# Differential attention in a two-layer trunk: GpSimd makes the subtraction factors, the reciprocals move between two maxima, a ScalarE copy moves between the exponentials

## The chip, the cores and the metric

The kernel runs on one core of one Trainium2 chip. The metric is the device time of one execution in microseconds (us). Its engines are named as the profile names them: PE (TensorE matmuls, PEld its weight loads), DVE (VectorE), ACT (ScalarE), POOL (GpSimd) and SP (the queue that issues the weight loads from HBM). Each engine runs its own list of instructions in order. They meet at semaphores.

## The reference

Two layers over 128 context tokens and 512 latent tokens, width 1024. Each layer has a token mixer with three parts side by side (6 heads of differential attention, a short convolution, 6 heads of latent attention, MLA below), and then a feed-forward part, dense in layer 0 and with experts in layer 1. The change is in the differential attention only:

```python
def diff_attention(q, k, v, lam):
    scale = DA ** -0.5                                # DA = 32, V_A = 64
    def block(qb):
        s = jnp.einsum('bqhcd,bkhcd->bhcqk', qb, k).astype(F32) * scale
        p = jax.nn.softmax(s, axis=-1)
        w = p[:, :, 0] - lam * p[:, :, 1]             # two softmaxes for each head
        return jnp.einsum('bhqk,bkhe->bqhe', w.astype(v.dtype), v)
    return sweep_query_blocks(block, q)
```

The kernel doesn't normalise the two softmaxes one by one. With sums S0 and S1 of the exponentials E0 and E1 it forms E0 + CNEG * E1, where CNEG = (1/S1) * S0 * (-lam), multiplies that by V, and scales the small output by 1/S0.

## The kernel before

**Items.** One loop over `k` from -2 to 60 runs in each layer on PE, ACT and DVE (`mixer_pe`, `mixer_act`, `mixer_dve`), with its own order of work on each. An item `j` is one head and one tile of 128 queries. Items 0 to 29 are differential (6 heads of 5 tiles, two scores each, c = 0 and 1). Items 30 to 59 are MLA heads with one score each. The tiles of a head come in the order 1, 2, 3, 4, 0. Tile 0 is the context: its scores have 128 columns, and those of a latent tile 640.

**The pipeline.** In step `k` an engine does its part for several items at once. PE: the scores of item k+2 (L1763), one group of transposes for the next head (`turn_group`, L1968), the product of item k-1 with V (L1791, 10 matmuls for a latent tile), the transposes of item k's weights (L1968, from `E`), and in one step of five a second group. ACT: the copy of the transposed group out of PSUM (`turn_out`, L759, into `QT` or `KT`), the two exponentials of item k+2 (L805), the copy `PT` (L810), and the copy of the second group where there is one. DVE: the two maxima of item k+2 (L1157), then for item k+1 the reciprocal `RC` (L1166), the factor `CNEG` (L1169) and the combination of `E` (L1171), then the scaling of item k-1's output (L1180), and after it work that is spread over certain steps (`latents_scale`, L1128, in steps 0 to 2 and 4 to 6, `latents_root` in step 3, `modulation_out` in step -1 of layer 0).

**What orders them.** There are two score buffers in PSUM. Score n waits until the exponential of score n-2 has given its sum (`exp_ready`), and a maximum waits for its score. All transposed groups of the attention go through one PSUM bank, so a group waits for the copy of the group before it (`turn_out`). The first score of a head waits for all six groups of that head. Groups 0, 1, 2, 4 and 5 are turned one in each step, in front of the product with V (`groups_at(k, 0)`), and group 3 in the third step of a head, at the step's end. Groups 0 to 2 come from the stack `QS`, 3 to 5 from `KS`.

**GpSimd.** POOL makes these stacks (`stack(h, k)`, L572 to L585): each is two casts and then two subtractions of the whole width. `QS` has two buffers, `KS` one, and a stack waits until the former contents have been turned. It also rotates the MLA queries and keys (`latent_rope`, L535 to L541). Its list is: stacks of head 0, query stack of head 1, ropes, key stack of head 1, the rope of the last key tile, and then the stacks of heads 2 to 5. That last rope waits for DVE's `latents_scale` of steps 0 to 2. In `Chain.then` an engine waits for its own instruction before it goes on.

## Time and profile before

| what | value |
|---|---|
| median of 3 runs | 2131.0 us (2129.53 to 2131.98) |
| the profiled execution, its own time | 2139.79 us |
| its span in the profile | 2137.8 us |
| busy over the span | PE 1907.5 us (89%), PEld 1719.2 us (80%), DVE 1417.2 us (66%), ACT 1031.7 us (48%), POOL 278.0 us (13%) |
| mean granted TensorE clock | 0.945 |

The differential items of layer 0 take the stretch from 217.92 to about 322 us, those of layer 1 start at 1168.88 us. The profiled execution is one of its own and was 8.8 us slower than the median of the runs. Busy shares are averages over stages that differ: PE is busy 89% of the whole span and less in the stretches of the change.

### The profile page before, as it was taken

To read this page: it belongs to the slowest core of one execution; us is meant where nothing else is said; L and a number is where in the kernel's file an instruction comes from. 1 tells how busy PE (TensorE), PEld (TensorE's weight loads), DVE (VectorE), ACT (ScalarE), POOL (GpSimd) and SP (SyncE) were. 2 spreads that over 40 slices of the span, in tenths; PEclk is the share of its full clock that TensorE was granted. 3 is DMA by queue.
4 is the path that set the end of the run, shared out by engine and by line. 5 is a ranking of instruction groups with operands and counts; after the bars stand their busy time and mean duration, and the time that the engine had idled before them with its cause. 6 is when DMAs were issued, how large, how long until landed. Compare 5 with 4: busy or idle time off the path is not lost.

```text
span 2137.8 us, 28644 instructions
## 1 busy us (share of the span) xinstructions
PE 1907.5 (89%) x11291; PEld 1719.2 (80%) x11291; DVE 1417.2 (66%) x2033; ACT 1031.7 (48%) x1388; POOL 278.0 (13%) x411
## 2 busy tenths in 40 slices
PE   5988789897999999997996889885699999999994
PEld 3986678797999999997985778774488888888883
DVE  5466784436665666546557884434589888898887
ACT  4235686413221121223235676414477777777772
POOL 0074310100111111000254311002000000000002
PEclk9999799798999999998997899987799999999997
DMA  8225200033555555421120000004789999999996
GB/s 325 66 75 201 79 1 1 20 99 99 175 176 163 170 164 185 127 89 39 57 94 26 1 1 1 1 1 176 296 349 384 405 390 404 392 400 397 376 396 225
DMA packets 115910, 375.64 MB, mean 176 GB/s; under 512 B 8640, under 2 KB 66400, under 8 KB 89408
## 3 DMA queue, kind: packets, MB, share of 16 engines
q1 hardware_dynamic: 94448, 303.50, 38.0%
q0 software_dynamic: 14240, 51.49, 7.1%
q10 hardware_dynamic: 7088, 18.81, 2.3%
q8 instruction: 91, 1.49, 0.3%
q14 instruction: 43, 0.35, 0.1%
HBM read 347.13 MB, written 26.64 MB: 175 GB/s over the span
## 4 chain that ended last, share of the span: by engine, by line
PE 75%; DVE 11%; ACT 8%; DMA 3%; issue 2%; POOL 1%; SPq 0%; ACTq 0%; DVEq 0%; POOLq 0%
PE PS L1988 31%; PE PS L1929 25%; PE PS L1968 5%; PE PS L1675 5%; PE PS L1791 4%; PE PS L1763 3%; ACT E L805 3%; ACT PT L810 1%; DMA rows_of_slots<-HTM,SLI 1%; DVE KCn L1128 1%; DMA araw<-in_w_ada_head 1%; DVE split L1402 1%; DVE SS L1111 1%; DMA raw<-in_w_ada_head 1%; DVE NT__177 L1458 1%
## 5 line engine op out<-in xcount | busy, mean ns | idle before, releaser
L1988 PE MATMUL PS<-H,split 128*128 128x320 f32 x2688 | 401.5, 312 | 10.3 <-DVE H L1595 8.0
L1988 PEld LDWEIGHTS PS<-H,split 128*128 128x128 f32 x2688 | 399.5, 190 | 12.5 <-issue 10.6
L976 ACT CAST split<-raw 128x2048 fp32r<-128x2048 f32 (+2 forms) x64 | 112.8, 1763 | 266.9 <-PE PS L1988 229.4
L1402 DVE TENSOR_TENSOR split<-raw,split 128x2048 fp32r<-128x2048 f32 (+2 forms) x64 | 138.0, 2161 | 129.6 <-ACT split L976 129.2
L1320 DVE TENSOR_TENSOR split<-raw,split 128x2048 fp32r<-128x2048 f32 x82 | 186.9, 2290 | 50.9 <-ACT split L931 50.9
L1320 DVE TENSOR_TENSOR msplit<-raw,msplit 128x2048 fp32r<-128x2048 f32 x82 | 187.8, 2292 | 32.7 <-ACT msplit L931 32.5
L1929 PE MATMUL PS<-split,HT 128*128 128x512 f32 x816 | 196.7, 397 | 5.4 <-DVE HT L1299 5.4
L1929 PE MATMUL PS<-msplit,HT 128*128 128x512 f32 x816 | 190.6, 389 | 0.0
L931 ACT CAST split<-raw 128x2048 fp32r<-128x2048 f32 x82 | 157.1, 1916 | 68.0 <-PE PS L1929 44.9
L931 ACT CAST msplit<-raw 128x2048 fp32r<-128x2048 f32 x82 | 156.9, 1914 | 64.6 <-PE PS L1929 64.6
L1675 PE MATMUL PS<-split,H 128*128 128x384 f32 (+1 forms) x960 | 170.2, 339 | 15.3 <-DVE split L1402 12.0
L1675 PEld LDWEIGHTS PS<-split,H 128*128 128x128 f32 x960 | 168.4, 194 | 17.0 <-DVE split L1402 13.2
L1929 PEld LDWEIGHTS PS<-split,HT 128*128 128x128 f32 x816 | 152.6, 190 | 36.6 <-DVE HT L1299 5.8
L1929 PEld LDWEIGHTS PS<-msplit,HT 128*128 128x128 f32 x816 | 153.2, 188 | 31.8
L1157 DVE TENSOR_REDUCE NM<-PS 128x1 f32<-128x640 f32 (+1 forms) x180 | 125.0, 714 | 71.8 <-PE PS L1763 70.0
L1988 PE MATMUL PS<-ACTB,split 128*128 128x320 f32 x1056 | 155.4, 309 | 0.0
L1988 PEld LDWEIGHTS PS<-ACTB,split 128*128 128x128 f32 x1056 | 155.0, 188 | 0.0
L805 ACT ACTIVATE E<-PS,NM 128x640 f32<-128x640 f32 (+1 forms) x180 | 126.8, 710 | 37.6 <-DVE NM L1157 37.5
L1511 DVE SCALAR_TENSOR_TENSOR DOTS<-DOTW,CROW 128x1024 f32<-128x1024 f32 x112 | 137.0, 1223 | 4.9
L1561 DVE SCALAR_TENSOR_TENSOR xT<-PS,MOD,xT 128x128 f32<-128x128 f32 (+2 forms) x120 | 43.5, 432 | 136.0 <-PE PS L1988 136.0
L1988 PE MATMUL PS<-MIX,split 128*128 128x320 f32 x768 | 117.2, 316 | 2.6 <-DVE MIX L1220 2.6
L1988 PEld LDWEIGHTS PS<-MIX,split 128*128 128x128 f32 x768 | 116.7, 194 | 3.1 <-DVE MIX L1220 3.1
(299 smaller groups left out, 2860.4 us busy)
## 6 DMA issues: line engine op xcount, KB each, us to landing
raw<-in_moe_w_gate SPq DMA_DIRECT2D x55, 1024.0 KB, 7.2
raw<-in_moe_w_down SPq DMA_DIRECT2D x55, 1024.0 KB, 8.1
raw<-in_moe_w_up SPq DMA_DIRECT2D x54, 1024.0 KB, 7.3
DOTW<-in_w_ada_rows POOLq DMA_DIRECT2D x56, 512.0 KB, 4.5
raw<-in_w_ada_head SPq DMA_DIRECT2D x16, 1024.0 KB, 6.8
mraw<-in_moe_w_up SPq DMA_DIRECT2D x14, 1024.0 KB, 7.2
mraw<-in_moe_w_gate SPq DMA_DIRECT2D x13, 1024.0 KB, 7.3
mraw<-in_moe_w_down SPq DMA_DIRECT2D x13, 1024.0 KB, 8.1
```

What stands on the lines that cost most here:

```text
L805: A.activation(out, src, ACT.Exp, bias=NM[:, m:m + 1], accum_out=SM[:, m:m + 1]).then_inc(S["exp_ready"], 1)
L931: A.copy(msplit[n % M_SPLIT][:, 0, :], mraw[n % M_RAW]).then_inc(S["pieces_hi"], 1)
L976: A.copy(split[u % 2][:, 0, 0:w], src[:, 0:w]).then_inc(S["split_hi"], 1)
L1157: V.tensor_reduce(NM[:, m:m + 1], src, op=ALU.max, axis=ax, negate=True).then_inc(S["max_ready"], 1)
L1320: V.tensor_tensor(msplit[n % M_SPLIT][:, 1, :], mraw[n % M_RAW], msplit[n % M_SPLIT][:, 0, :].bitcast(f32), ALU.subtract).then_inc(S["piec ...
L1402: V.tensor_tensor(split[u % 2][:, 1, 0:w], src[:, 0:w], split[u % 2][:, 0, 0:w].bitcast(f32), ALU.subtract).then_inc(S["split_lo"], 1)
L1511: ins = V.scalar_tensor_tensor(out=DOTS[:, :], in0=w[:, :], scalar=1.0, in1=CROW[:, v, :], op0=ALU.mult, op1=ALU.mult, accum_out=MOD[:, l, ...
L1675: ins = T.matmul(PS[:, m % 8, 0:w_], H[:, a, 4 * half + k, t * P:(t + 1) * P], W[:, w, k, :], start=(half == 0 and k == 0 and w == 0 and a ...
L1791: ins = T.matmul(PS[:, 0, 0:VA_W], PT[j % 2][:, i * P:(i + 1) * P], V[:, kt, col:col + VA_W], start=(i == 0), stop=(i == len(tiles) - 1))
L1929: ins = T.matmul(PS[:, bank + hf, :], A[:, a, 2 * j + k, :], W[:, w, first:first + 512], start=(j == 0 and k == 0 and a == 0 and w == 0), ...
L1968: return T.transpose(out, in_, ident[0:in_.shape[0], 0:in_.shape[0]])
L1988: ins = T.matmul(PS[:, 4 * (u % 2) + 2 * c + hf, 0:HALF], W[:, w, k, c * P:(c + 1) * P], A[:, a, k, hf * HALF:(hf + 1) * HALF], start=(k = ...
```

## The change

- **DVE.** The reciprocal of item k+1 (new function `invert`) stands between the two maxima of item k+2 in place of behind them, and DVE doesn't wait for its end; it signals the new semaphore `inverted`. In steps whose new item is an MLA item, `invert` stands for MLA items where the reciprocal stood. DVE no longer computes `CNEG`. It waits for the new semaphore `quotients` before the combination.
- **POOL.** It computes `CNEG` for each of the 30 differential items, when `inverted` allows. Between these, the stacks of heads 2 to 5 are made in halves: casts in one step, subtractions in the next. Keys of the coming head go with its first two steps, queries of the head after it with steps 3 and 4. The rope of the last key tile goes behind the factor and the half stack of step 3.
- **ACT.** The copy of the group in place 0 stands in front of the last exponential of item k+2. For two-score items this is between the two exponentials. For MLA items it is where it was.

```diff
--- before.py
+++ after.py
@@ -346,7 +346,7 @@
                  "setA_free setB_free proj_ready proj_free "
                  "nsq_ready nsq_used root_ready x_root eps_ready normed roped cache_loaded stores "
                  "ct_turned ct_hi ct_lo lat_ready lat_q lat_k subln_gained "
-                 "q_stacked k_stacked turned turn_out scored max_ready exp_ready w_ready pt_ready pt_out o_ready o_stored "
+                 "inverted quotients q_stacked k_stacked turned turn_out scored max_ready exp_ready w_ready pt_ready pt_out o_ready o_stored "
                  "subln_sq subln_sum subln_root subln_done mix_turned mix_hi mix_lo conv_hi conv_lo act_ready act_hi act_lo "
                  "router_loaded router_hi router_lo logits_ready logits_out top_ready top_exp gates_ready "
                  "crow_in crow_ready dot_used dots zeroed tables_ready h_rows_ready rows_turned rows_out mask_ready rank_ready slots_ready owners_ready scattered "
@@ -570,19 +570,21 @@
                 pool.dma_start(O["new_mla_ckv"][0, l], CN[:, 0, Q_RANK:Q_RANK + KV_RANK]).then_inc(S["stores"], 16)
                 pool.dma_start(O["new_mla_krope"][0, l], CN[:, 0, Q_RANK + KV_RANK:C_W]).then_inc(S["stores"], 16)
                 stores += 32
-                def stack(h, k):
+                def stack(h, k, halves=(0, 1)):
 
                     former = 6 * h if k else 6 * (h - 2) + 3
-                    if former > 0:
+                    if former > 0 and 0 in halves:
                         pool.wait_ge(S["turned"], l * TURNS + former)
                     buf, stack_, hi, lo = ((QA, QS[h % 2], (0, 2), (1, 3)), (KA, KS, (0, 1), (2, 3)))[k]
                     src = buf[:, :, h * 2 * DA:(h + 1) * 2 * DA].rearrange("p t (c d) -> p t c d", c=2)
-                    nc.gpsimd.tensor_copy(stack_[:, :, :, hi[1], :].bitcast(f32r), src)
-                    ch.then(nc.gpsimd.tensor_copy(stack_[:, :, :, hi[0], :].bitcast(f32r), src))
-                    for row in lo:
-                        ins = nc.gpsimd.tensor_tensor(stack_[:, :, :, row, :].bitcast(f32r), src,
-                                                      stack_[:, :, :, 0, :], ALU.subtract)
-                    ins.then_inc(S["k_stacked" if k else "q_stacked"], 1)
+                    if 0 in halves:
+                        nc.gpsimd.tensor_copy(stack_[:, :, :, hi[1], :].bitcast(f32r), src)
+                        ch.then(nc.gpsimd.tensor_copy(stack_[:, :, :, hi[0], :].bitcast(f32r), src))
+                    if 1 in halves:
+                        for row in lo:
+                            ins = nc.gpsimd.tensor_tensor(stack_[:, :, :, row, :].bitcast(f32r), src,
+                                                          stack_[:, :, :, 0, :], ALU.subtract)
+                        ins.then_inc(S["k_stacked" if k else "q_stacked"], 1)
 
                 def latent_rope(t, k):
                     pool.wait_ge(S["normed"], l * 21 + 2 * NT + 2 * t + k + 1)
@@ -601,10 +603,19 @@
                 latent_rope(NT - 1, 0)
                 pool.wait_ge(S["stores"], stores)
                 stack(1, 1)
-                latent_rope(NT - 1, 1)
-                for h in range(2, HEADS):
-                    stack(h, 0)
-                    stack(h, 1)
+                for k in range(-1, A_ITEMS - 1):
+                    j = k + 1
+                    m = 2 * (j % 3)
+                    pool.wait_ge(S["inverted"], l * A_ITEMS + j + 1)
+                    nc.gpsimd.tensor_scalar(CNEG[:, j % 3:j % 3 + 1], RC[:, m + 1:m + 2], SM[:, m:m + 1], LAM[:, l:l + 1],
+                                            ALU.mult, ALU.mult).then_inc(S["quotients"], 1)
+                    h, i = (k + 2) // NT + 1, (k + 2) % NT
+                    if 1 < h < HEADS and i in (0, 1):
+                        stack(h, 1, (i,))
+                    if 1 <= h < HEADS - 1 and i in (2, 3):
+                        stack(h + 1, 0, (i - 2,))
+                    if k == 3:
+                        latent_rope(NT - 1, 1)
 
                 pool.wait_ge(S["o_stored"], l * ITEMS + A_ITEMS)
                 for t in range(NT):
@@ -788,12 +799,13 @@
             root(HEADS, QK)
 
             for k in range(-2, ITEMS):
-                if (hg := groups_at(k, 0)) is not None:
-                    turn_out(*hg)
+                hg = groups_at(k, 0)
                 if k + 2 < ITEMS:
                     j = k + 2
                     cols = KEYS if TILE_ORDER[j % NT] else P
                     for c in range(comps_of(j)):
+                        if c == comps_of(j) - 1 and hg is not None:
+                            turn_out(*hg)
                         n = score_of(j, c)
                         bank, m = 2 + 2 * (n % 2), 2 * (j % 3) + c
                         act.wait_ge(S["max_ready"], l * SCORES + n + 1)
@@ -1143,6 +1155,17 @@
                         latents_scale(t - 1, 1)
                 latents_sums(t)
 
+            def invert(j):
+                m, n = 2 * (j % 3), comps_of(j)
+                dve.wait_ge(S["exp_ready"], l * SCORES + score_of(j, n - 1) + 1)
+                if j >= 3:
+                    dve.wait_ge(S["o_stored"], l * ITEMS + j - 2)
+                ins = V.reciprocal(RC[:, m:m + n], SM[:, m:m + n])
+                if n == 2:
+                    ins.then_inc(S["inverted"], 1)
+                else:
+                    ch.then(ins)
+
             for k in range(-2, ITEMS + 1):
                 if k + 2 < ITEMS:
                     j = k + 2
@@ -1156,18 +1179,15 @@
                             src, ax = PS[:, bank, 0:P], AX.X
                         V.tensor_reduce(NM[:, m:m + 1], src, op=ALU.max, axis=ax, negate=True).then_inc(
                             S["max_ready"], 1)
+                        if c == 0 and k >= -1 and comps_of(k + 1) == 2:
+                            invert(k + 1)
                 if 0 <= k + 1 < ITEMS:
                     j = k + 1
                     m, cols = 2 * (j % 3), KEYS if TILE_ORDER[j % NT] else P
-                    dve.wait_ge(S["exp_ready"], l * SCORES + score_of(j, comps_of(j) - 1) + 1)
-                    if j >= 3:
-                        dve.wait_ge(S["o_stored"], l * ITEMS + j - 2)
-                    n = comps_of(j)
-                    ch.then(V.reciprocal(RC[:, m:m + n], SM[:, m:m + n]))
-                    if n == 2:
-
-                        ch.then(V.tensor_scalar(CNEG[:, j % 3:j % 3 + 1], RC[:, m + 1:m + 2], SM[:, m:m + 1],
-                                                LAM[:, l:l + 1], ALU.mult, ALU.mult))
+                    if comps_of(j) == 1:
+                        invert(j)
+                    else:
+                        dve.wait_ge(S["quotients"], l * A_ITEMS + j + 1)
                         V.scalar_tensor_tensor(out=E[:, j % 3, 0, 0:cols], in0=E[:, j % 3, 1, 0:cols],
                                                scalar=CNEG[:, j % 3:j % 3 + 1], in1=E[:, j % 3, 0, 0:cols],
                                                op0=ALU.mult, op1=ALU.add).then_inc(S["w_ready"], 1)
```

## Rows read from the trace of the kernel before

**Rows 1.** By stretch: span; busy of PE, PEld, DVE, ACT, POOL; PEclk; DMA; GB/s.

```profile
217.92:237.36 19.44, 14.00 (x76) 11.74 (x77) 13.45 (x32) 12.71 (x29) 2.36 (x3) 0.68 0.68 216
237.36:260.30 22.94, 15.89 (x107) 14.09 (x105) 17.03 (x43) 13.07 (x31) 11.12 (x18) 0.85 0.00 1
...
276.02:291.75 15.73, 13.77 (x106) 11.92 (x105) 13.75 (x31) 12.76 (x31) 5.99 (x9) 1.00 0.00 1
```

**Rows 2.** Chain that ended last, stretch 218 to 345: start us, us, what.

```profile
293.05 0.58 ACT QT L759
293.63 1.57 ACT E L805 x4
...
296.28 0.58 ACT QT L759
```

**Rows 3.** Timeline of PE, stretch 288 to 332: start us, us, instruction [idle before].

```profile
292.42 0.60 PE L1968 MATMUL PS<-ident,QS 128*128 128x128 f32 x4
292.85 1.26 PE L1791 MATMUL PS<-VA,PT 128*128 128x64 f32 x10
293.94 0.71 PE L1968 MATMUL PS<-ident,E 128*128 128x128 f32 x5
294.48 0.56 PE L1763 MATMUL PS<-KT,QT 128*128 128x320 f32 x2
```

**Rows 4.** Timeline of DVE, stretch 300 to 332.

```profile
301.32 1.54 DVE L1157 TENSOR_REDUCE NM<-PS 128x1 f32<-128x640 f32 x2
302.79 0.15 DVE L1166 RECIPROCAL RC<-SM 128x2 f32<-128x2 f32 x1
302.98 0.27 DVE L1169 TENSOR_SCALAR CNEG<-RC,SM,LAM 128x1 f32<-128x1 f32 x1
303.29 0.89 DVE L1171 SCALAR_TENSOR_TENSOR E<-E,CNEG 128x640 f32<-128x640 f32 x1
304.12 0.28 DVE L1180 TENSOR_SCALAR QA<-PS,RC 128x64 f32<-128x64 f32 x1
```

**Rows 5.** Timeline of PE, stretch 215 to 262.

```profile
237.36 0.83 PE L1763 MATMUL PS<-KT,QT 128*128 128x320 f32 x4
242.63 1.11 PE L1968 MATMUL PS<-ident,QS 128*128 128x128 f32 x4 [4.44 <-POOL QS L583]
...
246.49 1.22 PE L1763 MATMUL PS<-KT,QT 128*128 128x320 f32 x4
```

**Rows 6.** Timeline of POOL, stretch 205 to 262.

```profile
237.91 0.73 POOL L535 TENSOR_TENSOR rope_c<-KCn,ROPE 128x96 f32<-128x96 f32 x2 [17.56 <-DVE KCn L1128]
...
240.91 1.67 POOL L583 TENSOR_TENSOR QS<-QA,QS 128x320 fp32r<-128x320 f32 x2
...
243.56 1.95 POOL L583 TENSOR_TENSOR KS<-KA,KS 128x384 fp32r<-128x384 f32 x2
...
246.37 1.70 POOL L583 TENSOR_TENSOR QS<-QA,QS 128x320 fp32r<-128x320 f32 x2
```

**Rows 7.** Timeline of DVE, stretch 215 to 262.

```profile
234.26 0.54 DVE L1128 SCALAR_TENSOR_TENSOR KCn<-KCn,RT,GR 128x96 f32<-128x96 f32 x2
...
246.23 0.17 DVE L1458 TENSOR_TENSOR NT__177<-RT 128x6 f32<-128x6 f32 x1
246.43 0.83 DVE L1459 SCALAR_TENSOR_TENSOR NT__177<-NT__177,SS 128x6 f32<-128x6 f32 x1
```

**Rows 8.** Timeline of ACT, stretch 215 to 262.

```profile
220.83 1.28 ACT L805 ACT_TABLE_LOAD   x1
```

**Rows 9.** Timeline of ACT, stretch 0 to 60.

```profile
20.09 1.28 ACT L1003 ACT_TABLE_LOAD   x1
25.65 0.21 ACT L1003 ACTIVATE XROOT<-XMEAN 128x5 f32<-128x5 f32 x1 [4.27 <-DVE XMEAN L1480]
```

**Rows 10.** Groups by line and shape, POOL, whole span: xcount, busy us, mean ns, idle before.

```profile
L535 POOL TENSOR_TENSOR rope_c<-QC,ROPE 128x96 f32<-128x96 f32 x16 | 6.0, 395 | 35.6 <-DVE QC L1128 35.6
...
L645 POOL MEMSET TIO<- 128x1 f32 x17 | 0.6, 98 | 0.0
```

## Prediction

> **What bounds the kernel now.** I read the page first (PE is the busiest engine of the whole span), then busy time by stretch, one head at a time, since the change touches 30 of the 60 items of each layer. A steady head lasts 15.73 us [rows 1]. PE is busy for 13.77 of it, DVE for 13.75, ACT for 12.76: nothing is full, so engines wait for each other in a circle. The stretch of the first head's items lasts 19.44 us with a granted clock of 0.68, the second 22.94 us, 7.2 more than a steady one.
>
> The chain shows the circle [rows 2]: group copy 0.58, exponentials with their sums 1.57, second score of the next item 0.56, group of transposes 0.43 [rows 3], hand-offs 0.1, and the next group copy: 3.24 us from one copy to the next. ACT waits for a group that PE can only turn behind a score, which waits for ACT's last exponential. PE's own work in such a step is 0.43 + 1.09 + 0.54 (starts that follow each other in [rows 3]) + two scores at 0.54 = 3.14 us. DVE's own is close as well: two maxima 1.47, reciprocal 0.19, `CNEG` 0.31, combination 0.83, scaling about 0.20, sum 3.00 [rows 4].
>
> The second head's loss has one large piece. PE stood still for 4.44 us before the first query group of head 2, until POOL's L583 ended [rows 5]. POOL had sat 17.56 us before the last key rope, and the stack stands behind that rope in its list [rows 6]. From the first score of that step to that of the next are 9.13 us [rows 5].
>
> **Part by part.** Per layer; the two layers have the same loop, and I take them as equal.
>
> *First head, ACT's table.* The load of the exponential's table takes 1.28 us at 220.83, behind the first group copy and directly in the path [rows 8]. With the copy moved, the exponential is the first instruction of the loop on ACT. A load doesn't wait for what its activation waits for: one ran at 20.09 and its activation came 4.27 us after the load, when DVE was ready [rows 9]. So it goes into idle time, and the first exponential also no longer stands behind the 0.58 copy. That is 1.28 + 0.58 plus the wait for the group, about 2.4 us at the first exponential; a bit more is won at the next two steps, where the old circle of copy and scores ran at a low clock, and some lost to POOL (below). Term: 2.5 (bounds 1.9 and 2.9).
>
> *Second head, the query stack.* The casts of head 2's queries are now made in step 0, the subtractions in step 1, and PE needs them in step 3; the rope no longer stands in front. The 4.44 us go. Next late in that step is DVE: maxima, combination and scaling to 2.5 us, then `latents_root`, 2.1 as it was (two operations near 0.8 and two near 0.2, with hand-offs [rows 7]), so that the step is about 4.6 in place of 9.13: minus 4.5. PE also keeps its clock (0.85 in this stretch, 1.00 in a steady one [rows 1]). In steps 4 and 6 POOL's subtractions now lie beside `latents_scale` (0.54 for its two operations [rows 7]), which can be held too, and I charge 1.0 back. Term: 3.5 (bounds 1.5 and 5.7).
>
> *Steady heads, ACT's copy and the reciprocal.* The old circle is gone: the copy's wait lies under an exponential of 0.785 (half of 1.57). A new circle goes from the end of a first score over the maximum 0.81, the exponential, the copy and the last exponential (together 2.15, as the chain shows) to the next item's second score: with three hand-offs of 0.04 it is 3.08 us, just under PE's 3.14. In the steps of a head where PE has less to do (a context tile in the product or in the scores) this circle is what is left; and group 3 waits for the copy of group 2, group 4 for that of group 3. Laid out so, the five steps are 3.14, 2.7, 3.05, 2.85 and 3.15: 14.9 us, a gain of 0.83 on 15.73.
>
> *`CNEG` on POOL.* No row shows this operation on POOL. From below it costs as a one-column memset, 0.098; the nearest with two inputs, 96 columns, takes 0.395 [rows 10]; on DVE it takes 0.27 [rows 4]. I take 0.3, nearest to DVE's and inside the pair, and keep 0.1 and 0.9 (three times) as bounds, since a per-partition scalar may be dear there. It starts 0.07 after the reciprocal and has the second maximum, 0.77, as cover: at 0.3 it costs nothing. Behind it DVE waits, with the combination, the scaling of the item before, and the next first maximum in line, for which ACT waits. DVE's step is then 0.77 + 0.15 + 0.11 + D + 0.84 + 0.20 = 2.07 + D if D outlasts the cover.
>
> *The stacks beside DVE.* This part can take the gain away. DVE's L1459 takes 0.83 us once, where POOL's subtraction at 246.37 runs, and its neighbour of the same width, L1458, takes 0.17 just before it begins [rows 6, 7]: an operation with two inputs in SBUF was held until POOL's ended. The combination of `E` is of that kind. Before, stacks came in bursts and a head met them once or twice; now each factor is followed at once by a piece, in four of five steps, and by POOL's order the piece starts just as the combination may. A key subtraction is 0.97 and a query one 0.84 (halves of [rows 6]). After the factor at 1.35 a key subtraction holds the combination from 1.73 to 2.35, so DVE's next maximum starts near 3.15 in a step whose other limits allow 2.7. That is 0.44 for each head, nothing for query and cast steps, which have some slack. Steady head: 15.3 us, gain 0.4; three such heads: 1.2 (bounds 2.5 without any hold, and minus 2.6 with a factor of 0.9).
>
> The Trainium skill (GPSIMD Engine Reference, Specifications) says that POOL shares its SBUF interfaces with VectorE and contends with instructions of two SBUF inputs. The 0.83 us above agree; by that rule alone every piece is a risk, without it the sum would be 23.8 in place of 16.2. The same page (Performance versus the Vector engine) has elementwise work about two times slower on POOL. An estimate by it from the 0.27: D = 0.53, and the sum would be about 13. No run here shows either for this operation.
>
> *Last differential head.* Three of its steps have MLA groups and the old circle; there are no stacks beside them. About 0.3 for each: 0.9 (bounds 0 and 1.0).
>
> *Nothing:* the order of `invert` for MLA items is the old one; the MLA steps, the feed-forward parts and the loads follow in time unchanged. DMA is at 0.00 in the stretches of the steady heads [rows 1], so nothing waits there that could swallow the gain.
>
> **Sum.** 2.5 + 3.5 + 1.2 + 0.9 = 8.1 for a layer, 16.2 for two. The profiled execution (2139.79 with its span of 2137.8) becomes 2123.6; it stands 8.8 above the median of the runs, which goes from 2131.0 to 2114.8.
>
> **The rivals.**
>
> *No hold (0.17).* POOL's instructions slip in between DVE's, as the short steps of a head leave gaps. For it: a maximum reads PSUM alone, and the gaps between POOL's two subtractions may let a combination in. Against: the 0.83. Terms 2.8 + 5.7 + 2.5 + 0.9 = 11.9, so 2107.
>
> *The stall moves (0.07).* In step 3 POOL has factor, casts and the rope (about 3.4 us), and the factor of item 5 comes late with the key subtractions behind it. The second head then gains 1.5 in place of 3.5: 2119.
>
> *A dearer factor (0.20).* D between 0.6 and 0.9. At 0.75 a key step is 0.77 + 0.26 + 0.75 + 0.97 + 0.67 (the combination once it is let in, 0.83 less a start of 0.16) + 0.2, near 3.6, a query step 3.45, and the steady head about 16.1: terms 2.4 + 2.5 - 1.2 + 0.3 = 4, so 2123; at 0.9, 2128.
>
> *Slower (0.11).* The wait for `quotients` takes the place of all others. From D = 1.0 the loss outweighs the two stalls that go. At 1.3 DVE's step is 3.4 without a piece and 4.1 with key subtractions, the steady head 17.9, three of them lose 6.4, the last head 2.3, and the first two keep 1.3 of their gain: minus 7.4 a layer, 2146. Against it stands the 0.395 of a 96-column operation.
>
> **How the numbers follow.** The forecast has 0.45, its own range is 2109 to 2119. Faster by over 0.2% (below 2126.7; about what a measurement of this kernel can tell from no change): 0.45 + 0.17 + 0.07 + 0.13 of the dearer factor = 0.82. Within it: 0.07 of that rival and 0.02 of the slower one, 0.09. Slower: 0.09. The range 2104 to 2127 holds all the faster cases.
>
> **What would show it.** Right: ACT's table load of L805 before the first group copy and idle time behind it; no wait of PE for `QS` L583; 15.3 us from first score to first score five items on; maxima of 0.81 with the reciprocal between; combinations of the key subtraction steps at 1.2 to 1.5 us. Wrong: a factor above 0.7 us on POOL, DVE idle before L1171 in every step, or PE waiting for `KS`.

## The result, and the profile after

| | before | after |
|---|---|---|
| median, both timed side by side | 2131.49 us (2129.53 to 2137.15, 4 runs) | 2108.59 us (2105.06 to 2111.09, 4 runs) |
| ratio of the times, 95% interval | | 0.987 [0.9829, 0.9912] |
| the profiled execution, its own time | 2139.79 us | 2105.06 us |
| its span | 2137.8 us | 2103.2 us |
| mean granted clock of that span | 0.945 | 0.953 |

The kernel became faster. The forecast was 2114.8 with a range of 2104 to 2127. The ratio, put on the 2131.0 of before, gives 2103.3, just under the range. Two later comparisons of the same two kernels gave 0.9898 [0.9852, 0.9945] and 0.9913 [0.9882, 0.9943]. All three together say 0.9 to 1.3%, where 0.76% was predicted.

The spans differ by 34.6 us. Reading both timelines from first score to first score, head by head, tells where:

| us | head 1 | head 2 | heads 3 to 5 | head 6 | differential items | MLA items |
|---|---|---|---|---|---|---|
| before, layer 0 | 19.44 | 22.94 | 15.72, 15.73, 15.73 | 14.55 | 104.11 | 94.96 |
| after, layer 0 | 16.36 | 16.99 | 15.00 each | 13.91 | 92.26 | 87.52 |
| before, layer 1 | 19.45 | 22.91 | 15.74, 15.73, 15.73 | 14.55 | 104.11 | 87.52 |
| after, layer 1 | 17.09 | 17.43 | 15.00, 15.00, 14.99 | 13.92 | 93.43 | 87.53 |

The items that the change touches give 11.85 + 10.68 = 22.5 us. The MLA items of layer 0 give another 7.4 and the work from there to layer 1's first score 4.5 (751.89 against 747.37). Both run the same code in both kernels; experiment 6 is about them. So 22.5 is the number to set against the predicted 16.2, and not 34.6.

Busy time by stretch of the changed kernel: the first head, the second, a steady one and the MLA items of layer 0, and the second head of layer 1 [rows 1].

```profile
217.81:234.17 16.36, 14.62 (x76) 12.90 (x77) 12.71 (x26) 11.42 (x28) 6.75 (x11) 0.63 0.80 256
234.17:251.16 16.99, 13.11 (x106) 11.77 (x105) 16.48 (x38) 13.03 (x33) 10.67 (x17) 1.00 0.00 1
266.16:281.16 15.00, 13.11 (x107) 11.77 (x105) 12.60 (x26) 12.69 (x31) 8.76 (x13) 1.00 0.01 2
310.07:397.59 87.52, 80.05 (x572) 67.90 (x570) 41.46 (x111) 52.29 (x112) 9.29 (x11) 1.00 0.04 13
...
1162.05:1179.48 17.43, 14.31 (x107) 13.26 (x105) 16.11 (x37) 12.85 (x31) 10.67 (x17) 0.90 0.01 1
```

DVE lost 1.15 us of work in a steady head (13.75 before), ACT next to nothing. The second head of layer 0 now holds the full clock; that of layer 1 has 0.90 (0.85 in both before).

ACT's timeline around its first exponential answers to [rows 8]. The table load stands before the first exponential, in idle time, and the group copy behind it:

```profile
216.33 1.28 ACT L817 ACT_TABLE_LOAD   x1
219.59 0.79 ACT L817 ACTIVATE E<-PS,NM 128x640 f32<-128x640 f32 x1 [1.98 <-DVE NM L1180]
...
220.38 0.58 ACT L770 CAST QT<-PS 128x512 fp32r<-128x512 f32 x1
```

The chain that ended last, in a steady head, answers to [rows 2]:

```profile
266.74 0.83 DVE NM L1180
...
267.60 0.88 ACT E L817 x2
268.49 0.48 ACT QT L770
268.96 0.80 ACT E L817 x2
269.76 0.04 issue
269.80 0.58 PE PS L1783 x2
...
270.40 0.82 DVE NM L1180
271.23 1.23 DVE E L1191
```

This is the circle of the prediction: maximum, exponential, copy, exponential, the other score. From 266.74 to 269.80 it takes 3.06 us (3.08 laid out). The wait for a transposed group is out of it. Behind it comes one combination on the path; DVE's timeline has it at 271.14 with 1.31 us, for 0.88 elsewhere.

Two pairs of rows from PE's timeline of the second head [rows 5]. The first and second row are the first scores of two steps that follow each other. The two below end the step that is long now; it began with the first score at 240.01:

```profile
234.17 0.83 PE L1783 MATMUL PS<-KT,QT 128*128 128x320 f32 x4
...
236.84 0.54 PE L1783 MATMUL PS<-KT,QT 128*128 128x320 f32 x2
...
244.70 0.63 PE L1988 MATMUL PS<-ident,KS 128*128 128x128 f32 x4 [1.97 <-ACT QT L770]
245.09 0.88 PE L1783 MATMUL PS<-KT,QT 128*128 128x320 f32 x4
```

The step that took 9.13 us takes 2.67. The 4.44 us wait for `QS` is gone, and a wait of 1.97 stands two steps later, in front of the first key group.

DVE's timeline there: the root's four operations [rows 7], and the combination and `latents_scale` of the long step.

```profile
237.27 0.17 DVE L1478 TENSOR_TENSOR NT__177<-RT 128x6 f32<-128x6 f32 x1
237.47 0.33 DVE L1479 SCALAR_TENSOR_TENSOR NT__177<-NT__177,SS 128x6 f32<-128x6 f32 x1
237.83 0.31 DVE L1480 SCALAR_TENSOR_TENSOR RT<-NT__177,RT 128x6 f32<-128x6 f32 x1
...
239.82 1.61 DVE L1191 SCALAR_TENSOR_TENSOR E<-E,CNEG 128x640 f32<-128x640 f32 x1
241.36 0.27 DVE L1200 TENSOR_SCALAR QA<-PS,RC 128x64 f32<-128x64 f32 x1
241.55 1.09 DVE L1140 SCALAR_TENSOR_TENSOR KCn<-KCn,RT,GR 128x96 f32<-128x96 f32 x2
```

POOL's timeline of the same time [rows 6]:

```profile
237.39 0.73 POOL L535 TENSOR_TENSOR rope_c<-KCn,ROPE 128x96 f32<-128x96 f32 x2
...
239.45 0.34 POOL L610 TENSOR_SCALAR CNEG<-RC,SM,LAM 128x1 f32<-128x1 f32 x1
239.75 2.55 POOL L585 TENSOR_TENSOR KS<-KA,KS 128x384 fp32r<-128x384 f32 x2
```

The first two operations of the root take 0.17 each and the last two 0.33 and 0.31, where the last two took about 0.8 before: POOL casts and ropes beside them and subtracts no stack. The factor of 239.45 comes late, because casts and rope stand in front of it in POOL's list, but it ends with DVE's second maximum (238.99 and 0.80 us), so that DVE hardly waits for it here. What costs time is that the subtractions that follow it begin just before the combination, which then takes 1.61 for its usual 0.88.

The new factor, its duration over all 60 of its kind (min/median/max), and who waited for it:

```profile
L610 POOL TENSOR_SCALAR CNEG<-RC,SM,LAM x60: 337/341/342, 222.5 to 1240.7; 128x1 f32<-128x1 f32 x60
...
  DVE E L1191: 4.4, 14
```

It costs 0.341 us, and DVE waited for it 4.4 us in all, 14 times. In the steady heads that is 0.29 in each step with a context tile (at 264.68 for example), where the two maxima that should cover it are short.

### The profile page after: what moved, and what is told of

Its sections match the earlier page's. It is cut to its first block, busy times and chain, and to the rows that moved or that the text cites. A ratio compares the mean times of both kernels' runs of the same rounds, so it can differ in the third digit from the quotient of the medians.

```text
span 2103.2 us, 28658 instructions
## 1 busy us (share of the span) xinstructions
PE 1888.6 (90%) x11291; PEld 1706.6 (81%) x11291; DVE 1402.6 (67%) x1973; ACT 1031.5 (49%) x1388; POOL 306.8 (15%) x471
## 4 chain that ended last, share of the span: by engine, by line
PE 76%; DVE 12%; ACT 5%; issue 3%; DMA 3%; POOL 1%; SPq 0%; POOLq 0%; ACTq 0%; DVEq 0%
PE PS L2008 32%; PE PS L1949 26%; PE PS L1695 5%; PE PS L1988 5%; PE PS L1811 4%; PE PS L1783 3%; ACT E L817 2%; DVE NM L1180 1%; ACT PT L822 1%; DMA rows_of_slots<-HTM,SLI 1%; DVE KCn L1140 1%; DMA araw<-in_w_ada_head 1%; DVE E L1191 1%; DVE SS L1123 1%; DVE split L1422 1%
```

## The experiments

Heads are given as first head / second head / steady head / last head, read as in the table above. One number for each stands for both layers where they agree within 0.1; otherwise layer 0 comes first. No kernel here moves the reciprocals alone: what their place is worth by itself stays open.

**1. The kernels again.** Both kernels unchanged, beside the others.

> The kernel before, unchanged. The two profiled executions differ by 34.6 us of span, of which 22.5 lie in the differential items (104.1 to 92.3 us in layer 0, 104.1 to 93.4 in layer 1); 7.4 lie in the MLA items of layer 0 (95.0 to 87.5 us), which the change doesn't touch, and 4.5 between there and layer 1's first score. Theory A (the rest is the granted clock of one execution): here the differential items again take 104.1 us in each layer, and the MLA stretch of layer 0 may be 87.5 like that of layer 1, with a granted clock of 1.00; the time is 2131 within 4. Theory B (the change also gives these 12 us, because its order keeps the clock up): the MLA stretch is again near 95 with a clock near 0.90.

> The kernel before once more, for its clock alone. Differential items 104 in each layer; MLA stretches were 95.0, 87.5, 88.7 and 87.5 in its two profiles. Belongs to the kernel: at least one again at 87.5 to 88.7; drawn anew: any.

> The changed kernel, unchanged. It was timed four times at 2105 to 2111. The MLA items took 87.5, 88.7 or 95 to 96.5 us in profiles of kernels that don't differ there. Theory A (one execution's granted clock, whatever the kernel): the differential items again take 92 to 94 us in each layer, the other stretches are drawn anew, and the median is the median before less 22 to 24. Theory B (the change keeps the clock up): both MLA stretches at 87.5 again, and the median 26 or more below.

> The changed kernel once more. Drawn anew: MLA stretches anywhere from 87.5 to 96.7 us, differential items 92 to 97, median 20 to 24 below the median before. Belongs to the kernel: 87.5 in most layers and 26 or more below.

Before against itself: 0.9994 [0.9971, 1.0016], 12 runs against 35. That is the width below which a time here tells nothing. Its items took 103.95 and 104.11 us in one profile, 103.99 and 104.17 in the other. The changed kernel gave the two ratios named above. Its medians lay 18.7 and 19.7 us under those of before, less than the 22 to 24 and 20 to 24 expected; the means of all executions lay 24.1, 22.1 and 20.9 apart in the three comparisons. Its items took 92.25 and 93.44 once more in the last, and 97.2 and 93.5 in the other, where the second and third head of layer 0 took 20.41 and 16.33, at a granted clock of 0.74 and 0.91. The items are the steadier measure, if one looks at the clock beside them.

**2. The copy alone.** The kernel before with ACT's part of the change, in two runs. In a further kernel only the very first copy (k = -2) is moved.

```diff
 for k in range(-2, ITEMS):
-    if (hg := groups_at(k, 0)) is not None:
-        turn_out(*hg)
+    hg = groups_at(k, 0)
...
         for c in range(comps_of(j)):
+            if c == comps_of(j) - 1 and hg is not None:
+                turn_out(*hg)
```

> The kernel before with ScalarE's copy moved alone. Theory A (the gain is a sum of separate terms): first exponential 2.2 us earlier by the hidden table load, stall for the query stack of head 2 unchanged at 4.4, steady head 15.73 to about 15.2 because VectorE's own 3.0 us of a step now decides, last head 0.6 less; 4 to 5 us for each layer, 2122. Theory B (the copy's circle was everything): steady heads at 15.0 and the sum near the full change less the stall, 2115. Theory C (nothing, VectorE was as full as the circle): only the table, 2127.

> The kernel before with the copy moved alone, once more. Belongs to the kernel: MLA stretches again at 95 to 96.5 in both layers, and no gain in the times (its items are 4.7 to 5.3 us shorter in each layer). Drawn anew: at least one below 92, and 5 to 10 us below the median before.

> The kernel before with the copy moved in its very first step alone. Theory A (the table load hides): first exponential 2.2 us earlier, the first head 19.44 to about 17.3, steady heads 15.73. Theory B (the next steps' circles eat it, since VectorE's or the clock's pace rules there): 18.5 or more.

Copy alone: 16.8 and 16.1 / 22.9 and 23.0 / 15.06 / 14.50. A second profile gave 16.7 and 17.2 / 22.4 and 22.9 / 15.07 / 14.50. So the copy makes 0.66 of the 0.73 us of a steady head, and all of the first head's gain; of the second head it makes nothing and of the last 0.05. Yet the ratios are 0.9997 [0.9972, 1.0022] and 0.9987 [0.9959, 1.0014], for some 10 us saved in the items: see 6. The first copy alone, in one execution: 17.55 and 18.20 / 23.75 and 22.33 / 15.73 / 14.56. The first copy, with the table load that it lets into idle time, is thus 1.9 and 1.3 of the first head, and the rest comes with the later copies. Of the 1.9, layer 0 gave 0.8 back in the second head, whose clock was 0.78.

**3. The query stack alone, with and without the copy.** The kernel before, with head 2's query stack ahead of the last key rope; the second kernel has the copy's edit too.

```diff
 stack(1, 1)
+stack(2, 0)
 latent_rope(NT - 1, 1)
 for h in range(2, HEADS):
-    stack(h, 0)
+    if h > 2:
+        stack(h, 0)
```

> The kernel before with GpSimd's query stack of head 2 ahead of the last key rope, nothing else. Theory A: the 4.4 us wait of PE and the half clock behind it go, the second head goes from 22.9 to about 17.5, 5 us for each layer, 2121; steady heads stay at 15.73. Theory B (the stall moves to VectorE's chain of latents_root or to the key stack): 20 us for the second head, 2125.

> The kernel before with two edits only: the copy moved, and the query stack of head 2 ahead of the last rope. Reciprocals, factors and whole stacks as before. Theory A (the two make nearly all of the gain): first head 16.1 to 16.8, second 18 to 19, steady 15.06, last 14.5, 9 to 10 us for each layer. Theory B (the two get in each other's way, the second head's holds by whole stacks grow): 7 or less.

Without the copy: 19.44 / 20.76 and 18.17 / 15.73 / 14.55, with 16.73 for one of layer 0's steady heads; ratio 0.9964 [0.9941, 0.9987]. With it: 16.7 and 17.4 / 19.16 and 20.91 / 15.08 / 14.50; ratio 0.9943 [0.9914, 0.9973]. The order alone takes out up to 4.7 us of the second head. Order and copy together save 8.5 us in the items of layer 0 and 6.1 in those of layer 1; the whole change saves 11.85 and 10.7, and its second head is 2.2 and 3.5 us shorter than theirs. The clock in those second heads was 0.82 and 0.76, against 1.00 and 0.90. How much of the difference is the clock and how much the burst of whole stacks stays open.

**4. The change without the copy.** The changed kernel with ACT's part taken back.

```diff
-hg = groups_at(k, 0)
+if (hg := groups_at(k, 0)) is not None:
+    turn_out(*hg)
...
-        if c == comps_of(j) - 1 and hg is not None:
-            turn_out(*hg)
```

> The changed kernel with ScalarE's copy back in front of both exponentials. Theory A: the second head keeps nearly all of its gain, the table load is in the path again (2.2 us), steady heads are at 15.7 or a little above, since the old circle of 3.24 us rules and the holds by GpSimd are added; 5 to 6 us for each layer are left of 11, 2120. Theory B (VectorE's shorter step is what counts): steady heads at 15.0, 2113.

19.45 / 16.87 / 15.73 / 14.57, ratio 0.9978 [0.995, 1.0006]. The chain of a steady head is the old one, with the same 1.57 and 0.58 [rows 2]:

```profile
271.86 0.58 ACT QT L770
272.45 1.57 ACT E L816 x4
274.02 0.04 issue
274.06 0.56 PE PS L1782 x2
274.62 0.45 PE PS L1987 x4
```

So relief for DVE is worth nothing there as long as the circle of ACT and PE sets the pace. Nor does a hold cost anything: in the same stretch two of its combinations took 1.52 and 1.38 us (at 275.42 and 281.46), and the head is no longer for it. All of this kernel's gain is in the second head: 6.05 us in both layers, more than in the changed kernel (5.95 and 5.48). Its clock was 1.00 there in both layers.

**5. The factor and the subtractions.** Four edits of the changed kernel. The factor is made twice on POOL; it is made on DVE, behind the second maximum, with POOL's pieces where they are; the key subtractions wait for the combination of the same step (a second kernel has the query ones wait too); or the subtractions of heads 2 to 5 are left out. The last leaves out part of the computation: heads 2 to 5 get stacks without their remainders, and the second cast gives the signal that the last subtraction gave.

```diff
# factor twice (POOL)
+ch.then(nc.gpsimd.tensor_scalar(CNEG[...], RC[...], SM[...], LAM[...], ALU.mult, ALU.mult))
 nc.gpsimd.tensor_scalar(CNEG[...], ...).then_inc(S["quotients"], 1)
# factor on DVE: POOL's instruction goes, and
-dve.wait_ge(S["quotients"], l * A_ITEMS + j + 1)
+dve.wait_ge(S["inverted"], l * A_ITEMS + j + 1)
+ch.then(V.tensor_scalar(CNEG[...], RC[...], SM[...], LAM[...], ALU.mult, ALU.mult))
# key subtractions wait; the other kernel: "or 1 <= h < HEADS - 1 and i == 3" as well
+if 1 < h < HEADS and i == 1:
+    pool.wait_ge(S["w_ready"], l * A_ITEMS + j + 1)
# no subtractions
...
-if 1 in halves:
+if 1 in halves and h < 2:
```

> The changed kernel with GpSimd computing each factor two times, one behind the other, so that it takes 0.75 us in place of 0.34. By the prediction's own sum (a step of VectorE at 2.07 + D, key step 0.97 more) the steady head goes up by 0.8. Theory A (the factor has cover except in the step of the key subtractions and of the context tile): up by about 0.4 to 0.5 for a head, 15.5. Theory B (cover everywhere): 15.0 to 15.1. Theory C (each step pays): 2 us a head, 17.

> The changed kernel with the factor back on VectorE, behind the second maximum, all else as changed (the pieces of the stacks are still paced by the reciprocals). Theory A (with the copy moved, VectorE has slack of its own and the factor's place is worth little): steady head 15.0 to 15.2, the first two heads within 0.5 of the changed kernel. Theory B (the 0.31 us for each step were needed): steady head up by 5 times 0.31, 16.5.

> The changed kernel with the key subtractions held back until VectorE has combined the weights of that step, so that they lie beside the scaling and the maxima. In the changed kernel the combination took 1.31 us there, 0.43 more than alone, and stood on the chain. Theory A (the hold costs what the chain shows): steady head 15.0 to 14.6, 3 us in all, at the edge of what the times can tell. Theory B (GpSimd is then late with the next factor, by about 0.4): 15.0 again or up to 15.4, the wait being moved from one engine to the other.

> The kernel whose key subtractions wait for the weights, once more. Belongs to the kernel: MLA stretches again at 96.6 in both layers. Drawn anew: at least one of them below 92. Steady heads 14.76 either way.

> As the run with the key subtractions held back, and the query subtractions too (their hold, 1.38 in place of 0.88 us, was not on the chain of the changed kernel). Theory A: no further gain from the queries, steady head as in that run. Theory B (GpSimd's list gets too long, factors late in two steps): 0.3 to 0.8 us more a head than that run.

> The changed kernel without the subtractions of the stacks of heads 2 to 5, so that the low parts of those heads' queries and keys are left over from earlier heads: a price of the hold, not a kernel of use. Theory A: the combination takes 0.88 us in each step, the steady head goes from 15.0 to 14.6, and the first two heads fall by 1 to 2 us each where latents_scale was held. Theory B (the hold is off the path): 15.0.

| us | first | second | its clock | steady | last | ratio |
|---|---|---|---|---|---|---|
| after | 16.36, 17.09 | 16.99, 17.43 | 1.00, 0.90 | 15.00 | 13.91 | 0.987, 0.9898, 0.9913 |
| factor twice | 16.76, 17.04 | 20.79, 20.99 | 0.84, 0.84 | 15.45 | 14.20 | 0.9959 [0.9934, 0.9983] |
| factor on DVE | 16.60, 17.13 | 20.05, 17.35 | 0.81, 0.90 | 15.64 | 14.23 | 0.9931 [0.9905, 0.9957] |
| keys wait | 16.33, 17.03 | 19.98, 17.54 | 0.83, 0.90 | 14.76 | 13.92 | 0.9914 [0.9890, 0.9938] |
| keys wait, again | 16.32, 17.12 | 19.81, 17.58 | 0.83, 0.90 | 14.76 | 13.92 | 0.9901 [0.9873, 0.9929] |
| all wait | 16.64, 17.04 | 19.74, 17.95 | 0.83, 0.90 | 14.76 | 13.91 | 0.9939 [0.9916, 0.9961] |
| no subtractions | 16.77, 17.09 | 15.37, 15.36 | 1.00, 1.00 | 14.76 | 13.92 | (one execution) |

Second heads near 20 us have a clock of 0.81 to 0.84, so they can't be set against the 16.99 of a clock of 1.00 as a price of the edit alone. The changed kernel itself took 20.41 at 0.74 once.

The factor twice, in the chain of a steady head: both factors and the combination in a row, on the path.

```profile
276.70 0.35 POOL CNEG L610
277.06 0.09 issue
277.14 0.35 POOL CNEG L612
277.50 0.03 issue
277.52 1.60 DVE E L1193
```

A factor of 0.35 + 0.09 + 0.35 = 0.79 us makes a steady head 0.45 longer, all of it in the key step (3.34 to 3.80). The working of the prediction's dearer factor (0.75 made a head 16.1 in place of 15.3) would have had 0.8: right in kind, too large, because the query step, laid out as growing too, stayed at 3.41.

The factor on DVE, in the chain of the key step:

```profile
275.28 0.19 DVE CNEG L1189
275.47 0.02 issue
275.49 1.65 DVE E L1191
```

The head is 0.64 longer, where at most 0.2 was expected; the key step goes from 3.34 to 3.99, more than the operation itself takes. The combination starts later, and then all of it lies under the subtractions. With whole stacks in bursts, the factor on DVE and the reciprocals in their old place (experiments 2 and 3) a steady head took 15.06 to 15.08. So the pieces and the moved reciprocals, with the factor left on DVE, are a loss of about 0.58, and with the factor on POOL they gain 0.06.

Without subtractions a steady head takes 14.76, so that the holds cost 0.24 there. Keys alone made to wait give the same 14.76, and the query ones nothing on top. In the second head the subtractions cost 16.99 - 15.37 = 1.6 in layer 0, at a clock of 1.00 with and without them, and 17.43 - 15.36 = 2.1 in layer 1, where the clock was 0.90 with them and 1.00 without. In the second head of layer 0, the chain of the kernel without subtractions shows what is left beside them, the factor behind the rope:

```profile
240.37 0.34 POOL CNEG L614
240.71 0.02 issue
240.73 0.89 DVE E L1195
```

Letting the key subtractions wait wins the 0.24 of a steady head, but no more. The chain there shows the key subtractions on the path themselves, and then the next factor, for which DVE waits 0.50:

```profile
276.33 1.97 POOL KS L585 x2
278.30 0.34 POOL CNEG L610
278.63 0.02 issue
278.66 1.03 DVE E L1193
```

The items of this kernel took 94.5 and 92.8 us (92.3 and 93.4 changed), with the second head of layer 0 at the low clock, and its ratios are those of the changed kernel. No version tried is shown to be faster than the changed kernel.

**6. What the clock adds.** No edit: the MLA items, whose operations no kernel here alters, in all the profiles. The stretch of layer 0 in two executions of the copy-only kernel:

```profile
318.44:414.98 96.54, 89.31 (x571) 76.33 (x569) 41.69 (x112) 52.41 (x112) 8.95 (x10) 0.88 0.04 12
```

```profile
316.61:404.15 87.54, 80.07 (x572) 67.87 (x570) 41.71 (x112) 52.35 (x112) 8.95 (x10) 1.00 0.04 13
```

The number behind POOL's (x10) is the granted clock: 0.88 and 1.00, and 9 us between them, with the same busy time on DVE, ACT and POOL. The stretch lasted 94.96 us before in layer 0, but 88.7 in two other profiles of that kernel; 87.5, 95.1 and 87.5 in three of the changed kernel; and 96.7 and 99.9 in the two of the one whose keys wait. So most of it is drawn anew with each execution, and the 7.4 us of the result were such a draw; the 4.5 behind them most likely too. Over 101 executions of the kernel before, the time went with the mean clock: 2128.12 us at 0.950, 2154.49 at 0.934; the slope inside the four sets was 1.6 to 1.8 us for 0.001. The fastest execution of before among all that were timed (2128.12) and the fastest of after (2105.06) stand 23.1 apart, near the 22.5 of the items. Their clocks are 0.950 and 0.953, and 0.003 is some 5 us by the slope. But an estimate from the items' own clocks (0.908 and 0.901 before, 0.934 and 0.910 after) has most of that 0.003 come from the changed items themselves, so it belongs to the change.

It also explains part of the copy-only kernel. Its timed runs had a mean clock of 0.939 and 0.941 beside 0.945 and 0.943 for before; at its own slopes of 1.1 and 1.6 us for 0.001, that is 7 and 4 us given away of the 10 saved. Whether a kernel can shift the odds of that draw stays open: the copy-only one and those with waiting subtractions leaned low (0.939 to 0.943), the changed one did not (0.945 and 0.946). Part of the lean of the latter is in the items: the second head of layer 0 was at 0.83 in all three of their profiles. For the rest there are too few profiles to say why.

## Why the prediction was right or wrong

The direction was right, and so were most of the mechanisms. Two terms of the sum were too small, and of the second head's term the working was wrong as well. Per layer:

| term | predicted | layer 0, layer 1 |
|---|---|---|
| first head | 2.5 | 3.08, 2.36 |
| second head | 3.5 | 5.95, 5.48 |
| three steady heads | 1.2 | 2.2, 2.2 |
| last head | 0.9 | 0.64, 0.63 |
| sum | 8.1 | 11.9, 10.7 |

*First head: right.* The load moved into idle time, and the first exponential no longer stands behind the copy. The first step went from 5.14 to 2.72 us, by the 2.4 forecast for it (by 2.2 in layer 1). The first copy alone gave 1.9 and 1.3 over the head (one execution), all copies the rest. The 3.08 of layer 0 is a little above the bound of 2.9.

*Second head: the step that failed.* The text put the step of 9.13 us at 4.6, "maxima, combination and scaling to 2.5 us, then `latents_root`, 2.1 as it was". It came out at 2.67 in layer 0 and 2.66 in layer 1: 6.5 gained, not 4.5. Two things were wrong with "as it was". The 0.83 and 0.80 of the root were themselves the hold by POOL's subtraction, which the text had read from the very same rows; with casts and rope beside it the four operations take 1.1 us with their hand-offs (237.06 to 238.14). And the root isn't in front of the next first score at all. Before, it was late because the scaling ahead of it waited 5.30 us for PE:

```profile
245.81 0.28 DVE L1180 TENSOR_SCALAR QA<-PS,RC 128x64 f32<-128x64 f32 x1 [5.30 <-PE PS L1791]
...
247.29 0.80 DVE L1460 SCALAR_TENSOR_TENSOR RT<-NT__177,RT 128x6 f32<-128x6 f32 x1
```

Even then the next first score started at 246.49, while the root still ran. The wait left with the stall. Now the root lies behind the next first score of 236.84, which needs only an exponential, and the step after that takes 3.17 where a steady one takes 2.92 (2.91 in layer 1). The charge of 1.0 was right as a net figure: the other four steps went from 13.81 to 14.32 (0.5) and from 13.79 to 14.77 (1.0). Most of it is in one step, 5.08 us long, where factor, rope and subtractions meet. The subtractions themselves cost 1.6 and 2.1, and the moved copy and factor gave part of it back. That PE keeps its clock held in layer 0 in two profiles of three; layer 1 had 0.90 in all three. The rival in which the stall moves named that place rightly (factor behind casts and rope, key subtractions behind it); its price is of the size of that 0.5 to 1.0, not 2.0 more.

*Steady heads: circle and hold right, two sizes off.* Laid out without a hold: 14.9; measured 14.76. Hold: 0.44 predicted, 0.24 measured, in the key step alone, as predicted. The five steps run at 2.66, 2.92, 3.34, 3.41 and 2.67 us, against 3.14, 2.7, 3.05, 2.85 and 3.15. The 3.14 for PE's own step was a wrong number: it took two scores at 0.54 each from [rows 3], where a pair of matmuls stands by itself. Four in a row need 0.68 from their start to the next operation's (266.16 to 266.84), so that PE's step is 2.66. The rows of before already spoke against 3.14: from the head's first score at 291.75 (the end of the last stretch in [rows 1]) to the next at 294.48 [rows 3] are 2.73 us. The other way round, the fourth step was laid out at 2.85 and took 3.41; its chain goes over `PT` and the group copy behind it (275.34 to 276.42) before PE can turn the next group. Without the hold the third step is 3.11. So the five errors are -0.5, +0.2, +0.1, +0.6 and -0.5, and that they add up to only -0.1 is luck. The share of the parts: copy 0.66, factor on POOL and reciprocals between the maxima, together and with no subtraction beside them, 0.31 (15.07 to 14.76; the copy-only kernel of the 15.07 has its stacks in bursts), subtractions minus 0.24. Relief of DVE without the copy gives 0.00.

*Last head: right in size, 0.64 for 0.9.* But the copy alone gives 0.05 and the rest of the change without it nothing. It takes both: with the circle opened, DVE is next.

*The factor: right.* 0.341 us for 0.3, nearest to DVE's 0.27 as assumed. The Trainium skill (GPSIMD Engine Reference, Performance versus the Vector engine) has elementwise work about two times slower on POOL; what it measured is an add of two tensors with 2048 columns. The traces do not show that ratio for an operation of one column: 0.341 to 0.27 is 1.3 times; an estimate by that rule would have made the sum 13, further off.

*The range* gave the case without holds 0.17 and 2107. Measured, the holds exist (1.6 in the second head of layer 0, 0.24 in steady ones), so its mechanism is false, though its 23.8 in all stands nearer to 22.5 than the forecast's 16.2: the steps beside the holds were shorter than laid out. From 2131.0 the measured 22.5 leads to 2108.5, inside the range. The first comparison's 2103.3 lies 5 us lower, and the two later ones (0.9898, 0.9913) lead to 2109.3 and 2112.5. So what most likely carried the first one over the edge was the clock of four executions (0.947 to 0.953, where the fifteen later ones have 0.945 in the mean), for which the range had no allowance. With 5.7 for the second head the forecast would have been 2110.4, among the three comparisons.

## What to carry to other kernels

When a stall is taken out, read what is late next from the dependences of the next instruction that matters, not from the list of what used to run there, and don't carry a duration over that the text itself has just explained by contention. Relief of an engine is worth nothing until the circle that sets the pace is opened: here the copy's place made 0.66 us of a steady head and the relief alone 0.00, while in the last head neither counted without the other. And for changes below one per cent, compare stretches of profiles whose granted clock is the same; whole times carried 10 us and more of clock.

## What the runs showed of the hardware

- **Holds by POOL.** A DVE operation with two inputs in SBUF that meets a POOL subtraction is held up, whatever its own size: 128x6 took 0.83 for 0.31 to 0.33, 128x640 took 1.31 to 1.65 for 0.88. A hold works both ways: POOL's pair of key subtractions took 1.97 when DVE's combination was kept out of its start (the waiting kernel), and 2.54 beside it. Maxima and the reciprocal kept their 0.80 to 0.82 and 0.15 beside all of this. The Trainium skill (GPSIMD Engine Reference, Specifications) says that POOL shares its SBUF interfaces with VectorE and contends with its instructions of two SBUF inputs. The traces agree, and add that it costs 0.24 us in a steady head and 1.6 in the second head of layer 0.
- **The granted clock differs between executions of one code.** PE stood idle 1.84 us for the same `PT` before the same product with V in both profiles (371.90 before, 359.93 after). Before, it fell some 2 us later to the lower of its two levels (1.2 GHz of 2.4): four MLA scores took 2.34 us at 377.85. After, it did not, and the same four took 1.24 at 364.31.

```profile
371.90 1.33 PE L1791 MATMUL PS<-VC,PT 128*128 128x64 f32 x10 [1.84 <-ACT PT L810]
...
377.85 2.34 PE L1763 MATMUL PS<-LT 96*128 96x320 f32 x4
```

```profile
359.93 1.33 PE L1811 MATMUL PS<-VC,PT 128*128 128x64 f32 x10 [1.84 <-ACT PT L822]
...
364.31 1.24 PE L1783 MATMUL PS<-LT 96*128 96x320 f32 x4
```

The code and the gap are the same, and so are PE's rows of the 8 us ahead of it. What tells the two apart stays open. The second heads in the profile of the changed kernel show it too: the wait of 1.97 in front of the key group is the same in both layers, and the four scores behind it take 0.88 us in layer 0 (245.09) and 1.42 in layer 1 (1173.05).
- **Short matmuls in a row.** A pair of 320-column scores shows 0.54 to 0.56 us and four show 0.83, of which 0.68 pass until the next operation starts. A sum of such rows overstates what PE needs.
